# Root mean squares by row, memory turns behind the first projection, and an earlier place for local attention's exponentials

## The reference, cut to what matters

```
h    = x * rsqrt(mean(x*x, -1) + 1e-6) * ln1_gain            # 264 tokens
proj = h @ w_in                                              # q/k/v, delta rule, memory q, 3 x 1024 gates
mem  = mem_prompt * rsqrt(mean(mem*mem, -1) + 1e-6) * mem_norm   # 256 memory tokens
k, v = split(mem @ w_mem_kv)
# sliding-window attention, 8 query heads, 2 key/value heads, window 128, ALiBi, a learned sink
s = q k^T / 8 - slope*dist, masked; p = softmax([s, sink])[:-1]; o = p v
```

## Time and profile before

| | |
|---|---|
| runs, median | 1404.99 us (three: 1404.38 to 1406.32) |
| profiled execution | 1404.77 us, span of its instructions 1402.4 us |
| TensorE busy | 1346.7 us (96%) |
| VectorE, ScalarE busy | 435.8 us (31%), 275.9 us (20%) |
| read from HBM | 459.09 MB, 332 GB/s over the span |
| granted TensorE clock | 1.000 |

### The profile page before, as it was taken

The page is one execution under the profiler, slowest core; times in us unless marked ns, Lnnn a source line. Parts: engine busy times, 40 slices in busy tenths (PEclk is TensorE's granted clock), DMA queues, the critical chain, the costliest instruction groups (busy, mean ns, idle before and its releaser), DMA issues.

```text
span 1402.4 us, 17627 instructions
## 1 busy us (share of the span) xinstructions
PE 1346.7 (96%) x6392; PEld 700.7 (50%) x6392; DVE 435.8 (31%) x1164; ACT 275.9 (20%) x562; POOL 23.4 (2%) x53
## 2 busy tenths in 40 slices
PE   8999999999999999999999999999999999999998
PEld 6887777897677333433333333333333433334333
DVE  4036252545832213322132121322213322132222
ACT  4232724212313210111111101111110111101111
POOL 3000000000000000000000000000000000000000
PEclk9999999999999999999999999999999999999999
DMA  8744322213598689999999999999999999999995
GB/s 262 251 161 150 95 65 87 65 61 114 185 344 366 278 330 419 426 427 425 426 428 426 427 426 425 427 426 427 426 424 427 428 426 426 425 425 428 427 425 216
DMA packets 84696, 464.47 MB, mean 331 GB/s; under 512 B 5523, under 2 KB 41469, under 8 KB 51712
## 3 DMA queue, kind: packets, MB, share of 16 engines
q1 hardware_dynamic: 82960, 458.28, 80.6%
q0 software_dynamic: 1520, 5.40, 1.3%
q10 hardware_dynamic: 176, 0.22, 0.1%
HBM read 459.09 MB, written 5.83 MB: 332 GB/s over the span
## 4 chain that ended last, share of the span: by engine, by line
PE 75%; DMA 18%; ACT 3%; DVE 3%; issue 1%; SPq 0%; DVEq 0%; ACTq 0%
PE bank L682 70%; DMA ring<-in_w_mlp 18%; PE bank L686 5%; ACT arena L1641 0%; DMA arena<-in_x_prompt 0%; ACT arena L1400 0%; ACT arena L1537 0%; DVE arena L2202 0%; ACT ring L1422 0%; ACT arena L1536 0%; ACT L1400 0%; DVE arena L2208 0%; DVE arena L2211 0%; DVE arena L1944 0%; ACT arena L1402 0%
## 5 line engine op out<-in xcount | busy, mean ns | idle before, releaser
L682 PE MATMUL bank<-ring,arena 128*64 128x512 f32 (+3 forms) x3264 | 709.2, 581 | 32.7 <-DMA ring<-in_w_mlp 22.8
L682 PEld LDWEIGHTS bank<-ring,arena 128*64 128x64 f32 (+2 forms) x3264 | 236.2, 138 | 458.8 <-issue 383.2
L682 PE MATMUL bank<-arena 128*128 128x264 f32 (+17 forms) x1272 | 303.6, 394 | 8.9 <-ACT arena L1400 1.7
L682 PE MATMUL bank<-arena,ring 128*128 128x264 f32 (+1 forms) x1136 | 263.6, 387 | 2.5 <-ACT ring L1422 1.2
L682 PEld LDWEIGHTS bank<-arena 128*128 128x128 f32 (+7 forms) x1272 | 173.0, 179 | 132.2 <-issue 90.8
L682 PEld LDWEIGHTS bank<-arena,ring 128*128 128x128 f32 x1136 | 210.2, 190 | 45.7 <-issue 11.0
L2190 DVE COPY arena<-bank 128x512 f32<-128x512 f32 x32 | 22.1, 692 | 532.1 <-PE bank L682 532.1
L686 PEld LDWEIGHTS bank<-arena 128*128 128x128 f32 (+5 forms) x712 | 86.5, 168 | 60.4 <-issue 54.3
L686 PE MATMUL bank<-arena 128*128 128x128 f32 (+5 forms) x712 | 108.4, 287 | 8.1 <-DMA arena<-in_x_prompt 6.0
L1678 ACT ACTIVATE arena<-bank 128x512 f32<-128x512 f32 x32 | 19.1, 597 | 393.5 <-PE bank L682 393.5
L1674 ACT ACTIVATE arena<-bank 64x512 f32<-64x512 f32 x63 | 37.2, 591 | 148.6 <-PE bank L682 147.8
(11 more groups left out here) (326 smaller groups left out, 424.8 us busy)
## 6 DMA issues: line engine op xcount, KB each, us to landing
ring<-in_w_mlp SPq DMA_DIRECT2D x126, 2048.0 KB, 23.2
ring<-in_w_mlp SPq DMA_DIRECT2D x128, 1024.0 KB, 19.6
ring<-in_w_in SPq DMA_DIRECT2D x25, 1024.0 KB, 5.2
ring<-in_w_branch SPq DMA_DIRECT2D x6, 1024.0 KB, 9.7
ring<-in_w_mem_kv SPq DMA_DIRECT2D x4, 1024.0 KB, 16.1
ring<-in_cache_mem_k SPq DMA_DIRECT2D x4, 1024.0 KB, 5.3
ring<-in_cache_mem_v SPq DMA_DIRECT2D x4, 1024.0 KB, 7.0
ring<-in_w_out SPq DMA_DIRECT2D x4, 1024.0 KB, 9.6
```

Of the source, the lines that this page charges most:

```text
L682: return nc.tensor.matmul(out, lhsT, rhs, start=start, stop=stop, skip_group_check=True)
```

## The change

1. Sums of squares. Lines 1425 to 1440 go. ScalarE squares the rows as loaded (token on the partition), with `accum_out` giving the row sums: sample, two halves of the prompt, then two halves of the memory. Roots are taken with `Sqrt`, reciprocals on VectorE. TensorE spreads the result over the partitions by a product of the broadcast column with the identity (`rs_b`, `mem_b`). Both `layer_sums` are gone.
2. Copies. VectorE copies all eight blocks of `xT`; the turned memory isn't copied, but scaled straight out of banks 5, 7, 2 and 3 (two blocks each).
3. Order. TensorE: nine products of ones before the prompt has landed, prompt transposes, parameters, `rs_b`, projection 0, memory broadcast and memory transposes, projections 1 to 3, state transposes, memory products. SP: ring piece 0, memory rows, ring pieces 1 to 7, with no wait for parameters or state.
4. Local attention. ScalarE does the exponentials first and then copies out late 10 to 13. Late 12 and 13 use banks 0 and 1 (once the scores have left them). Late 14 moves behind the attention, in two parts, in place of two of the `stay_awake` fillers (one and three products); ScalarE copies it out behind the turned keys.

```diff
@@ sync
         sp.dma_start(x_nat, ...)
-        sp.dma_start(mem_nat, A["mem_prompt"][0].rearrange("(c p) d -> p c d", p=P)).then_inc(sem("mem_landed"), 16)
-        sp.wait_ge(*at("prm_landed", 160))
-        sp.wait_ge(*at("cst_landed", 16))
         for i, dmas in enumerate(pieces):
+            if i == 1:
+                sp.dma_start(mem_nat, A["mem_prompt"][0].rearrange("(c p) d -> p c d", p=P)).then_inc(sem("mem_landed"), 16)
@@ tensor
+        for _ in range(9):
+            mm(B[7][:, 0:P], ones, ones)
...
-        for g in range(16):
...
-        layer_sums(0, T, G_flat)
+        for k in range(KD):
+            if k >= 4:
+                pe.wait_ge(*evacuated(k - 3))
             for c in range(2):
+                tr(B[k % 4][:, P * c:P * c + P], x_nat[:, c, P * k:P * k + P])
+            tr(B[k % 4][:, 2 * P:T], xs_nat[0:NB, P * k:P * k + P]).then_inc(sem("x_T"), 1)
         pe.wait_ge(*at("prm_landed", 160))
         tr(B[7][:, 0:76], prm[0:76, :]).then_inc(sem("prm_T"), 1)
-        layer_sums(1, NP_TOK, cv_flat)
+        pe.wait_ge(*at("rs_inv", 1))
+        for c, (a, n) in enumerate(TOK):
+            ins = mm(B[4][:, a:a + n], rs_col[0:n, c:c + 1].broadcast_to([n, P]), ident[0:n, 0:n])
+        ins.then_inc(sem("rs_b"), 1)
+        def turn_mem():
+            pe.wait_ge(*at("mem_landed", 16))
+            pe.wait_ge(*at("rsm_inv", 1))
+            for c in range(2):
+                ins = mm(B[4][:, P * c:P * c + P], rs_col[:, 3 + c:4 + c].broadcast_to([P, P]), ident)
+            ins.then_inc(sem("mem_b"), 1)
+            pe.wait_ge(*at("colp_ready", 1))
...
+                    ins = tr(B[MEM_BANKS[k // 2]][:, a:a + P], mem_nat[:, c, P * k:P * k + P])
...
-        for n in range(4):
-            project(n // 2, n % 2, n, hT)
+        pe.wait_ge(*evacuated(8))
+        project(0, 0, 0, hT)
+        turn_mem()
+        project(0, 1, 1, hT)
         pe.wait_ge(*at("memTn_ready", 8))
+        for n in range(2, 4):
+            project(1, n % 2, n, hT)
...
-        attend("sw", 8, (10, 11, 12, 13, 14), sw_scores, sw_values, sw_turn)
-        stay_awake(B[3], 1, T)
+        attend("sw", 8, ((10, None, None), (11, None, None), (12, None, 7), (13, None, 8)), sw_scores, sw_values, sw_turn)
+        late(14, after=10, blocks=range(0, 2))
         pe.wait_ge(*at("sw_o", 4))
+        pe.wait_ge(*at("late_out", 14))
...
-        stay_awake(B[3], 3, T)
+        late(14, blocks=range(2, 8))
@@ scalar
+        fn(rs_col[:, 5:6], eps_col, ACT.Sqrt)
+        act.wait_ge(*at("xs_landed", 16))
+        fn(squares[2][0:NB, :], xs_nat[0:NB, :], ACT.Square, accum_out=rs_col[0:NB, 2:3])
+        act.wait_ge(*at("x_landed", 16))
+        for c in range(2):
+            ins = fn(squares[c], x_nat[:, c, :], ACT.Square, accum_out=rs_col[:, c:c + 1])
...
+        fn(rs_col[:, 0:2], rs_col[:, 0:2], ACT.Sqrt, bias=eps_col, scale=1.0 / D).then_inc(sem("ln_rt"), 1)
+        act.wait_ge(*at("mem_landed", 16))
+        for c in range(2):
+            ins = fn(squares[3 + c], mem_nat[:, c, :], ACT.Square, accum_out=rs_col[:, 3 + c:4 + c])
...
+        act.wait_ge(*at("mem_b", 1))
+        fn(rsm, B[4][:, 0:NP_TOK], ACT.Copy).then_inc(sem("rsm_ready"), 1)
...
-        late_to_sbuf(10, 11)
...
-        late_to_sbuf(12, 13, 14)
+        late_to_sbuf(10, 11, 12, 13)
@@ vector
+        for k in range(KD):
+            dve.wait_ge(*at("x_T", k + 1))
+            v.tensor_copy(xT[:, k, :], B[k % 4][:, 0:T]).then_inc(sem("x_evac" if k < 5 else "x_late"), 1)
+            if k == 4:
+                dve.wait_ge(*at("ln_rt", 1))
+                v.reciprocal(rs_col[0:NB, 2:3], rs_col[0:NB, 2:3])
+                v.reciprocal(rs_col[:, 0:2], rs_col[:, 0:2]).then_inc(sem("rs_inv"), 1)
```

More of the change, by code:

```diff
@@ L97 @@
 CHAINS = {
-    "pe_load": [("x_T", 16), ("prm_T", 1), ("cst_T", 1)],
+    "pe_load": [("x_T", 8), ("prm_T", 1), ("rs_b", 1), ("mem_b", 1), ("mem_T", 4), ("cst_T", 1)],
     "pe_small": [("ab_ps", 1), ("ab_nT", 1), ("kmT_ps", 2), ("conv_rows_ps", 3)],
@@ L206, in build_program @@
     stat = take(160)
+    rs_col = take(6)
     xT_flat, hT_flat = take(KD * T), take(KD * T)
@@ L237, in build_program @@
     mem_nat = grid(cols(scr, 3072, 2048), D)
-    memT = grid(cols(oT_flat, 0, 2048), NP_TOK)
+    squares = [cols(oT_flat, D * i, D) for i in range(3)] + [cols(G_flat, D * i, D) for i in range(2)]
     memTn = grid(cols(cv_flat, 0, 2048), NP_TOK)
-    rsx, rsm = cols(Kn_flat, 0, T), cols(Kn_flat, 512, NP_TOK)
+    rsm = cols(Kn_flat, 512, NP_TOK)
     cst_nat = cols(region_q, 0, 1536)
@@ L741, in project, with late @@
             ins.then_inc(sem("proj"), 1)
-        def late(n, after=None, blocks=range(KD)):
+        def late(n, after=None, blocks=range(KD), scores=None):
             if blocks[0] == 0:
@@ L748, in late @@
                     pe.wait_ge(*at("late_out", after + 1))
+                if scores is not None:
+                    pe.wait_ge(*at("sw_s_evac", scores))
             w = grid(slot(PC_LATE[n // 2]), 256)
@@ L843, in attend @@
                 scores(i, B[i % 2]).then_inc(sem(tag + "_s"), 1)
-            for i in between:
-                late(i, after=i - 2 if i > between[1] else None)
+            for i, after, evacuated_scores in between:
+                late(i, after=after, scores=evacuated_scores)
             for i in range(n):
@@ L935, in _ @@
             if b < 7:
-                late(15, after=13, blocks=[b])
+                late(15, after=11, blocks=[b])
         ins.then_inc(sem("ss_s"), 1)
-        late(15, after=13, blocks=[7])
+        late(15, blocks=[7])
         pe.wait_ge(*at("ss_sT", 1))
@@ L1763, in _ @@
         dve.wait_ge(*at("colp_ready", 1))
-        step(v.tensor_scalar(column(C_QS), column(C_QS), HD_S ** -0.5, None, ALU.mult))
+        dve.wait_ge(*at("rs_b", 1))
+        for k in range(KD):
+            v.scalar_tensor_tensor(hT[:, k, :], xT[:, k, :], column(LN1 + k), B[4][:, 0:T], ALU.mult,
+                                   ALU.mult).then_inc(sem("hT_ready"), 1)
+        dve.wait_ge(*at("ln_rt", 2))
+        v.reciprocal(rs_col[:, 3:5], rs_col[:, 3:5]).then_inc(sem("rsm_inv"), 1)
+        step(v.tensor_scalar(column(C_QS), column(C_QS), HD_S ** -0.5, None, ALU.mult))
+        dve.wait_ge(*at("rsm_ready", 1))
+        for k in range(KD):
+            dve.wait_ge(*at("mem_T", k // 2 + 1))
+            a = NP_TOK * (k % 2)
+            v.scalar_tensor_tensor(memTn[:, k, :], B[MEM_BANKS[k // 2]][:, a:a + NP_TOK], column(LNM + k), rsm, ALU.mult,
+                                   ALU.mult).then_inc(sem("memTn_ready"), 1)
         dve.wait_ge(*at("const_ready", 3))
```

77 lines of the change are left out of this document (25 added, 52 removed).

## The result

The changed kernel takes 1399.35 us at the median (five runs, 1394.91 to 1401.93), against 1404.99 before (five runs, 1404.38 to 1406.32): a ratio of 0.9956, interval 0.9946 to 0.9967. It is faster, by 5.6 us between the medians where 9.6 were forecast, and its median lies 0.75 us above the range. The profiled execution took 1394.91 us, 0.3 from the forecast. One run of the study, of the variant with the start alone, took 2325.95 us at a mean granted clock of 0.555, and that variant's median is given without it.

The account below looks back on a forecast made before the run. TensorE's chain was taken to bound the kernel, with a weight stream saturated in the experts that moves with it. Start 7.7 plus attention 1.9 gave 9.6 us, so 1395.2 us, range 1392.6 to 1398.6.

Parts of the forecast that it names:

- What bounds the kernel: Whole kernel: TensorE's chain, then a weight stream saturated in the experts; a microsecond won ahead counts fully at the end.
- F: Rival at the experts: stream already saturated ahead of the last release, so the gain vanishes and time stays 1404.8; chance 0.04.
- The start: Up to the memory products: dropped sums of squares and new order bring them from 38.93 to 31.2 us, 7.7 gained.
- clock up throughout: Start: fillers lift TensorE's clock and it stays up, 8.7 us gained, 1394.2 in all; chance 0.22.
- case B: Start: fillers lift the clock, it falls, the first projection regains it; 1.0 us lost, 7.7 gained, 1395.2; chance 0.42.
- D: Rival at the start: a weight piece late at 22 or 31 us, 3 us of stall, 1398.2; chance 0.10.
- E: Rival at the start: parameter rows starve behind SP's queue, memory products 11 us later, 1414; chance 0.03.
- The attention: Local attention: exponentials start earlier, turns come 3.05 us sooner, part given back, net 1.9 us.
- The fifth gate behind the attention: Late 14 moved behind the attention: two blocks cost 0.1 ahead of a wait, six blocks 1.05.
- The clock: Start: TensorE read as at 1.2 GHz until about 17.1 us; fillers may lift it, costing nothing or up to 0.5.
- Three cases follow: Start: clock lifted and stays up (8.7 us gained), lifted and falls (7.7), or not lifted (5.6).
- Case C: Start: fillers don't lift the clock, memory products at 33.3 us, 5.6 us gained, 1397.3 in all; chance 0.19.

Follow-up runs that it names:

- the start alone: The change's start (sums, order, fillers) with the old local attention, against the kernel before: 1401.3 us over seven runs, ratio 0.9968.
- the fourth execution: The changed kernel unedited, run a fourth time for one profiled execution: 1393.33 us.
- the repeated execution: Profiled execution of the changed kernel run again without edit; that group of six runs has median 1395.78 us, ratio 0.9939.
- the attention alone: The change's local attention part with the old start, against the kernel before: 1402.74 us over eleven runs, ratio 0.9982.
- the grouped turns: Changed kernel with the eight sample-row transposes done together ahead of the prompt's: 1396.19 us, ratio 0.994.

## Why the prediction was right or wrong

**What bounds the kernel: right.** Over the fourteen traces the span behind the expert mark lies between 893.2 and 894.6 us while the mark itself moves from 498.28 to 512.32. A microsecond won ahead of the experts is one at the end, within that 1.4 us, and the saturated stream (F) swallows none of it.

**The start: right in its parts.** With the clock up throughout I had the first mark at 30.25; the fourth execution has 30.31, with some 0.4 us of its turns still at the lower level. With case B I had 31.2; the profiled and the repeated execution have 31.64 and 31.96. The reciprocals and the broadcast are within 0.3 us of where I had them. One part was read too short: quick turns were to be over near 9 us, with TensorE idle to 12.7 but for `rs_b`; they took to 10.45, and the idle time was 0.98 us. It cost nothing, since ScalarE's squares and roots take as long. No weight and no parameter was waited for in the four traces of the changed kernel, so D and E did not happen; the slack of D's second piece was 4 us in the profiled one where I had 2.

**The attention: the mechanism right, one term mis-sized.** The turns come 3.10 us earlier (3.05 forecast). The fifth gate behind the attention cost 1.56 where the steps had 1.15: the two blocks ahead of the wait cost 0.44 for 0.10, the six behind it 1.12 for 1.05. The net is 1.54 for 1.9, and the attention alone confirms it with 1.61.

**The clock: this step failed.** "Three cases follow" was right as a list: all three were seen from one start code. Four things in it were wrong.

1. I made the likeliest case the time. The case isn't a property of the code but of the execution: first marks 30.31, 31.64, 31.96, 33.00 and 35.64. The old start has no such spread in its two traces (38.93, and 38.87 with the new attention); its clock was low up to the same point in both.
2. Case C was priced at a gain of 5.6. It measured 3.29 and, without fillers, 3.38. I had the clock back at 17.1 us, where it rose in the old kernel in the sums of squares, which the change removes. In case C it rose at about 21: the first projection began at 15.16 and not 14.5, and took 6.78 us and not 4.9.
3. Case B's loss of 1.0 us was 1.3 to 2.7 (first marks less 30.31), or 1.7 to 3.0 by the length of the first projection (5.49 and 6.84 us less 3.81).
4. Falls later in the kernel weren't in the sum at all. The one profiled execution of before had none, so no view of it showed them. They were met between 198 and 213, 238 and 251, and 347 and 357 us, in seven of thirteen new traces, with the old start as well (244 to 250 us in the attention alone). Two short ones cost 1.6 to 1.7 us each, one of some 7 us ahead of a wait 1.4, and the longest, of some 10 us, 3.5. The runs of the kernel before, in groups of 19, 11 and 11, spread over 4.2 to 5.3 us each, with mean granted clocks down to 0.992, so it has them as well, and a good part of the spread is not the change's.

The thirteen runs of the changed kernel together go from 1393.33 to 1401.93, with 1396.61 in the middle. The first median, 1399.35, had a mean granted clock of 0.995 against 0.998 in the profiled one, so it spent more time at the lower level; which of the falls it had, no record says. Nor does the mean tell all: the slowest run, 1401.93, reads 0.998, and a start that isn't lifted leaves no mark in it (1.000 in the start alone). A sum made from one execution gives one value of a distribution nearly 9 us wide, and the range, 6 us, was built around that one value with C mispriced. With C at its measured gain (3.3 us at the first mark, 1.5 for the attention) the rival C comes to 1400.0, above the range. The middle of the thirteen lies inside it, so that the first five runs fell outside has chance in it too.

**What decides whether the clock rises or stays** isn't settled. It isn't the kind of instruction alone (in one execution products didn't lift it, in another transposes did). The gaps probably matter: with both filled, the first projection ran at 3.81 us in three of three traces, and with them open in one of the six traces in which the clock had risen before them. But the fourth execution kept its level through the same gaps, and nine traces are few.

## What to carry to other kernels

A start made shorter with fillers and short waits left TensorE's clock to chance per execution here; price the spread over executions, and look at several traces before you call one of them the time. Filling such gaps with products kept the level at the start in three traces, but the medians don't yet tell it from leaving them open. Order the work so that a stage fits at either level where you can: the grouped turns did. Read the clock from the durations of one form of instruction, not from the granted clock alone. A gain in front of a saturated stream counted in full here, where each of the stream's releases comes from the engine that gained.

## What the runs showed of the hardware beyond that

- The granted clock reads 1.00 up to its first recorded change, even where instructions take twice their time: 25 transposes in 6.95 us at "1.00" against 4.60.
- 18 us of almost dense products with an identity or with ones left the clock at 1.2 GHz in one execution. Of the nine traces with nine products of ones as fillers it was up during the prompt's turns in six (25 turns in 4.48 to 5.02 us, 3.39 grouped) and not in three (6.95, 4.61 grouped, and that one).
- In the run of 8-row transposes between 128-row ones the turns take longer than with the 8-row ones grouped in front: 4.60 us against 3.39 at the upper level.
- The one fall of the clock seen in the expert stage (944 us) cost under 0.3 us, with the waits for the weights behind it; the later falls measured ahead of the experts cost 1.4 to 3.5 us.
